# A two-layer transformer trunk on one core: the work ahead of the first projection rebuilt

## What is computed

```python
def ada_modulate(c, w, b):
    m = jax.nn.silu(c) @ w + b
    shift, scale, gate = jnp.split(m, 3, axis=-1)
...
        shift, scale, gate = ada_modulate(c, ada_w[i, 0], ada_b[i, 0])
        h = rms_norm(x, norm_g[i, 0]) * (1.0 + scale) + shift
        ...
            mix = even_mixer(h, rel_bias, ev_w_in[j], ev_w_out[j], ...)
        x = x + gate * mix
```

## Time and profile before

| | us |
|---|---|
| median of 3 runs | 2055.22 |
| lowest and highest run | 2053.96 and 2059.96 |
| span of the profiled execution (first to last instruction) | 2054.0 |
| TensorE busy in it | 1889.3 (92%) |
| VectorE busy in it | 1559.5 (76%) |
| ScalarE busy in it | 1057.0 (51%) |
| first product of `ev_in` starts at | 124.4 |

### The profile page before, as it was taken

One profiled execution on the slowest core, in us unless ns is written; L12 is line 12 of the kernel. 1 busy time (PEld: TensorE's weight loads), 2 busy tenths in 40 slices (PEclk: granted clock), 3 DMA queues, 4 the chain that ended last, 5 costly groups with the idle time before them and its releaser, 6 DMA issues.

```text
span 2054.0 us, 34033 instructions
## 1 busy us (share of the span) xinstructions
PE 1889.3 (92%) x11434; PEld 1629.2 (79%) x11434; DVE 1559.5 (76%) x2447; ACT 1057.0 (51%) x2257; POOL 220.1 (11%) x317
## 2 busy tenths in 40 slices
PE   3279998889999999999999999989999999999998
PEld 2158854766799999997877878777799999998787
DVE  4988744777778888889887888788677777778554
ACT  1145446655544545555544456565455555556443
POOL 2220001552100000000011000043000000000000
PEclk9689998999999999999999999999999999999999
DMA  8979985567588888886997886868567777765555
GB/s 325 399 278 320 339 295 170 198 229 245 200 278 281 270 273 277 278 272 231 331 332 266 271 282 203 301 220 300 193 232 224 225 234 235 224 203 177 177 189 176
DMA packets 210967, 521.25 MB, mean 254 GB/s; under 512 B 23041, under 2 KB 43010, under 8 KB 186018
## 3 DMA queue, kind: packets, MB, share of 16 engines
q1 hardware_dynamic: 180722, 316.19, 47.3%
q0 software_dynamic: 28032, 201.44, 26.9%
q10 hardware_dynamic: 2096, 2.12, 0.3%
HBM read 517.53 MB, written 2.12 MB: 253 GB/s over the span
## 4 chain that ended last, share of the span: by engine, by line
PE 73%; DVE 13%; DMA 9%; ACT 3%; issue 1%; SPq 0%; DVEq 0%; POOLq 0%; ACTq 0%
PE ps L1039 12%; PE ps L1035 12%; PE ps L1036 12%; PE ps L931 10%; PE ps L927 10%; PE ps L928 10%; DVE acc L1712 6%; DVE ring_lo L1790 3%; DMA ring<-in_od_w_in 2%; DMA first_ring<-in_ada_w 2%; DMA ring<-in_ev_w_in 1%; DMA aring<-in_ada_w 1%; PE ps L761 1%; PE ps L1131 1%; DVE L L1947 1%
## 5 line engine op out<-in xcount | busy, mean ns | idle before, releaser
L1242 ACT ACTIVATE ring_hi<-ring 128x512 fp32r<-128x512 f32 (+2 forms) x1152 | 690.8, 621 | 595.5 <-DMA ring<-in_ffn_w_up 231.6
L1790 DVE TENSOR_TENSOR ring_lo<-ring,ring_hi 128x512 fp32r<-128x512 f32 (+2 forms) x1152 | 742.3, 680 | 283.1 <-ACT ring_hi L1242 281.4
L1035 PE MATMUL ps<-hT_hi,ring_hi 128*128 128x256 f32 x2048 | 512.2, 283 | 1.5 <-PE ps L1039 0.7
L1036 PE MATMUL ps<-hT_lo,ring_hi 128*128 128x256 f32 x2048 | 507.2, 280 | 0.0
L1036 PEld LDWEIGHTS ps<-hT_lo,ring_hi 128*128 128x128 f32 x2048 | 387.3, 189 | 0.0
L1035 PEld LDWEIGHTS ps<-hT_hi,ring_hi 128*128 128x128 f32 x2048 | 384.7, 188 | 2.3 <-issue 1.2
L1039 PE MATMUL ps<-hT_hi,ring_lo 128*128 128x256 f32 x2048 | 329.2, 282 | 2.4 <-DVE ring_lo L1790 2.4
L1039 PEld LDWEIGHTS ps<-hT_hi,ring_lo 128*128 128x128 f32 x2048 | 279.2, 187 | 2.6 <-DVE ring_lo L1790 2.6
L1712 DVE SCALAR_TENSOR_TENSOR acc<-aring,cs,acc 128x2048 f32<-128x2048 f32 x112 | 263.4, 2352 | 20.6 <-DMA aring<-in_ada_w 8.8
L928 PE MATMUL ps<-ring_hi,hT_lo 128*128 128x512 f32 (+2 forms) x640 | 243.8, 382 | 0.0
L643 POOL DMA_DIRECT2D aring<-in_ada_w x176 | 94.4, 536 | 1380.7 <-DVE acc L1712 1355.6
(11 more groups left out here) (244 smaller groups left out, 1996.4 us busy)
## 6 DMA issues: line engine op xcount, KB each, us to landing
aring<-in_ada_w POOLq DMA_DIRECT2D x176, 1024.0 KB, 6.9
ring<-in_ffn_w_up SPq DMA_DIRECT2D x512, 256.0 KB, 3.0
ring<-in_ffn_w_down SPq DMA_DIRECT2D x256, 256.0 KB, 3.1
ring<-in_od_w_in SPq DMA_DIRECT2D x112, 256.0 KB, 3.5
ring<-in_ev_w_in SPq DMA_DIRECT2D x80, 256.0 KB, 5.8
first_ring<-in_ada_w POOLq DMA_DIRECT2D x16, 1024.0 KB, 7.2
ring<-in_ev_w_out SPq DMA_DIRECT2D x64, 256.0 KB, 3.5
ring<-in_od_w_out SPq DMA_DIRECT2D x64, 256.0 KB, 4.0
```

Source lines behind the costliest of these rows:

```text
L1035: nc.tensor.matmul(o[q], hi, hT_hi[:, kt, :], start=start, stop=False, skip_group_check=True)
L1036: nc.tensor.matmul(o[q], hi, hT_lo[:, kt, :], start=False, stop=False, skip_group_check=True)
L1242: ins = nc.scalar.activation(out_, in_, f, **kw)
L1790: put(v.tensor_tensor(ring_lo[:, g, part], ring[:, g, part], ring_hi[:, g, part].bitcast(F32), ALU.subtract), lo_ok)
```

## The change

The condition is loaded first on SP and straight as columns (2048 elements of 4 bytes), so that silu(c) needs no turning. GpSimd issues the first four units ahead of the clearing of `acc`. The bias is no longer made with `toeplitz`: the table is split into a high and a low float32r part, stacked to 64 rows, and for each of the 256 key positions a product of 16 columns with a shifted slice of the one-hot table writes one column per head; eight float32 products of 512 columns add the causal mask. The scratch tensor, its two DMAs, `k_neg` and the flipped identity go. SP waits until unit 30 has landed before it issues the first ring buffer. Units 28 to 31 are multiplied by TensorE straight from their buffers, after the column sums of the other 28, into the same accumulators. VectorE's loop is written out, the copies of the parameters stand after unit 7, and the normalised x is made by ScalarE.

```diff
-        FIRST_MOD = 2 * KT
+        FIRST_MOD, DIRECT = 2 * KT, 4
...
+        def first_used(n):
+
+            return first_mod(n) - DIRECT
...
-            row_load(0, ROWS["c"][0], c.rearrange("o (k p) -> (o k) p", p=P))
+            sp.dma_start(cs[:, :], c.rearrange("o (k p) -> p (o k)", p=P), allow_slow_non_contiguous=True).then_inc(c_in, 16)
+            sp.dma_start(hot, k_hot).then_inc(buckets_in, 16)
+            for half in range(2):
+                sp.dma_start(tbl[half * BUCKETS:(half + 1) * BUCKETS, :], rel_bias).then_inc(buckets_in, 16)
...
-            for dst, src in ((con[:, :], k_con), (fold4, k_fold), (hot, k_hot), (negrow, k_neg), (tbl, rel_bias),
+            for dst, src in ((con[:, :], k_con), (fold4, k_fold),
...
+            _, landed_, turn = mod_slot(FIRST_MOD - 2)
+            sp.wait_ge(landed_, 16 * (turn + 1))
             for j, (c0, n) in enumerate(EV_BLOCKS):
                 matrix(KT * j, ev_w_in[0], KT, c0, n)
...
+            for m in range(4):
+                load(m, -1, m % 2, m // 2)
             clear(-1, (0, 1))
-
-            def first_pass(i):
-                for j in range(4):
-                    load(j, -1, j % 2, i * 2 + j // 2, i * 4)
-            first_pass(0)
-            with pool.Fori(1, KT // 2) as i:
-                first_pass(i)
+            for m in range(4, FIRST_MOD):
+                load(m, -1, m % 2, m // 2)
...
-            pe.wait_ge(params_in, 16 * 8)
+            pe.wait_ge(params_in, 16 * 5)
...
-            ins = nc.tensor.matmul(ps[0:SLOTS, 2, 0:REV], tbl[:, :], hotr, start=True, stop=True)
-            lane.done(ins, rev_mm)
-
+            pe.wait_ge(hot_ok.handle, 1)
+            pe.wait_ge(tbl_ok.handle, 2)
...
                     ins = nc.tensor.matmul(ps[:, 3, (t * NCMP + j) * NSA_H:(t * NCMP + j + 1) * NSA_H],
-                                           hotf[:, d0:d0 + P], tbl[:, 0:NSA_H], start=True, stop=True)
+                                           hot_r[:, d0:d0 + P], tbl_r[:, 0:NSA_H], start=True, stop=True)
...
-            pe.wait_ge(toep_in, 16)
-            pe.wait_ge(prm_ok.handle, 4)
-            pe.wait_ge(cb_ok.handle, 1)
-            for b in range(8):
-                ins = nc.tensor.matmul(ps[:, b, :], con[:, C_FLIP:C_FLIP + P], wide[:, b * 512:(b + 1) * 512], start=True, stop=True)
-            lane.done(ins, flipped)
+            def bias_bank(b):
+
+                nc.tensor.matmul(ps[:, b, :].rearrange("p (s h) -> p s h", h=SLOTS), ident,
+                                 causal[:, b * 32:(b + 1) * 32].unsqueeze(2).broadcast_to([P, 32, SLOTS]), start=True, stop=False,
+                                 skip_group_check=True)
+                for s in range(32):
+                    d0 = FWD0 + P - (b * 32 + s)
+                    ins = nc.tensor.matmul(ps[:, b, s * SLOTS:(s + 1) * SLOTS], hot_r[:, d0:d0 + P], tbl_r[:, :],
+                                           start=False, stop=s == 31, skip_group_check=True)
+                lane.done(ins, bias_mm)
+
+            for b in BIAS_BANKS:
+                if b == 0:
+                    pe.wait_ge(prm_ok.handle, 4)
+                if b == 3:
+                    pe.wait_ge(cb_ok.handle, 1)
+                bias_bank(b)
             pe.wait_ge(bias_ok.handle, 8)
...
-                    pe.wait_ge(ada_used.handle, first_mod(n) - 1 + t)
+                    pe.wait_ge(ada_used.handle, first_used(n) - 1 + t)
...
-                                               acc[:, t, j * NB:(j + 1) * NB], start=True, stop=True)
+                                               acc[:, t, j * NB:(j + 1) * NB], start=True, stop=n > 0)
+                if n == 0:
+                    pe.wait_ge(cs_ok.handle, 1)
+                    for m in range(FIRST_MOD - DIRECT, FIRST_MOD):
+                        t, k = m % 2, m // 2
+                        slot, landed_, turn = mod_slot(m)
+                        pe.wait_ge(landed_, 16 * (turn + 1))
+                        for j in range(4):
+                            ins = nc.tensor.matmul(ps[32 * j:32 * j + 1, sums_bank(n) + t, :], cs[:, k:k + 1], slot[:, j * NB:(j + 1) * NB],
+                                                   start=False, stop=k == KT - 1)
...
-            act.wait_ge(ones_ok.handle, 1)
-            act.wait_ge(prm_ok.handle, 4)
-            run(cs_ok, cs[:, :], prm[:, ROWS["c"][0]:ROWS["c"][0] + KT], ACT.Silu)
-
-            act.wait_ge(rev_ok.handle, 1)
-            act.dma_start(toeplitz, rev).then_inc(toep_out, 16)
+            act.wait_ge(c_in, 16)
+            run(cs_ok, cs[:, :], cs[:, :], ACT.Silu)
+            act.wait_ge(buckets_in, 48)
+            run(hot_ok, hot_r, hot, ACT.Copy)
+            run(tbl_ok, tbl_r, tbl, ACT.Copy)
+
             act.wait_ge(x_in, 16)
             for b in range(4):
                 x_squares(b, hT)
             x_norm(0)
-            act.wait_ge(toep_out, 16)
-            act.dma_start(wide[:, 0:SLOTS * S].rearrange("p (h s) -> p h s", h=SLOTS),
-                          bass.AP(toeplitz.tensor, 0, [[1, P], [REV, SLOTS], [1, S]])).then_inc(toep_in, 16)
-            act.wait_ge(flipped.handle, 1)
-            for b in range(8):
-                run(bias_ok, bias[:, 2 * b:2 * b + 2, :], ps[:, b, :].rearrange("p (h s) -> p h s", h=2), ACT.Copy)
+            act.wait_ge(xsd.handle, 2)
+            for b in range(4):
+                cols = slice(b * NB, (b + 1) * NB)
+                for t in range(ST):
+                    run(xn_ok, xn[:, t, cols], x_sb[:, t, cols], ACT.Copy, scale=xst[:, 0, t:t + 1])
+            for i, b in enumerate(BIAS_BANKS):
+                act.wait_ge(bias_mm.handle, i + 1)
+                run(bias_ok, bias[:, :, b * 32:(b + 1) * 32], ps[:, b, :].rearrange("p (s h) -> p h s", h=SLOTS), ACT.Copy)
...
-            dve.wait_ge(cs_ok.handle, 1)
...
-                def one_pass(i):
-                    lane.after()
-                    put(v.tensor_copy(cs_now[:, 0:2], cs[:, 0:2] if isinstance(i, int) else cs[:, bass.ds(i * 2, 2)]))
-                    for j in range(4):
-                        mod_unit(j, j % 2, cs_now[:, j // 2:j // 2 + 1], i * 4)
-                one_pass(0)
+                def units(m0, m1):
+                    for m in range(m0, m1):
+                        mod_unit(m, m % 2, cs[:, m // 2:m // 2 + 1])
+
+                dve.wait_ge(cs_ok.handle, 1)
+                units(0, 1)
+                dve.wait_ge(tbl_ok.handle, 1)
+                put(v.tensor_tensor(tbl_r[BUCKETS:, :], tbl[BUCKETS:, :], tbl_r[BUCKETS:, :].bitcast(F32), ALU.subtract), tbl_ok)
+                units(1, 8)
...
+                dve.wait_ge(prm_T.handle, 1)
+                for a, b in ((0, ROWS_A), (PE_COL, PE_COL + 2 * CMP_BLOCK), (CW_COL, 4 * P), (4 * P, PRM)):
+                    put(v.tensor_copy(prm[:, a:b], ps[:, a // 512, a % 512:a % 512 + b - a]), prm_ok)
...
+                units(8, 12)
                 normed(0)
-                with lane.loop(1, KT // 2, {ada_used: 4, dve_s: 1}, ada_used) as i:
-                    one_pass(i)
+                units(12, FIRST_MOD - DIRECT)
...
+                if n == 0:
+                    return
                 lane.after()
                 for b in range(4):
-                    for t in range(ST if n == 0 or b >= 2 else 1):
+                    for t in range(ST if b >= 2 else 1):
```

54 lines of the change are left out of this document (21 added, 33 removed).

## The result

| | before | after |
|---|---|---|
| median (4 runs each, same chip) | 2054.7 us | 2043.76 us |
| lowest and highest run | 2053.96 and 2059.96 | 2040.8 and 2050.84 |
| span of the profiled execution | 2054.0 | 2049.1 |
| first product of `ev_in` | 124.4 | 115.4 |
| from there to the end of the span | 1929.6 | 1933.7 |

The ratio is 0.9943 with a 95% interval of 0.9921 to 0.9966, that is 7.0 to 16.2 us. A second session with 7 and 19 runs gave 0.9944, 0.9917 to 0.9971 (2045.79 against 2055.51), and there the first product stood at 116.0. The profiled execution of the changed kernel is its slowest of the first four; the other spans were 2042.8, 2041.3 and 2039.1. So the prologue is read by its first product, and the span of that one execution is not used.

A forecast was written before the change was run, and what follows sets the result against it. TensorE's bias work was to set the prologue's end: 22.5 + 1.8 + 6.5 + 68.8 = 99.6 us, then 0.5 + 2.6 + 7.4 + 0.3 = 110.4 against 117.4. Saving 7.0 gave span 2047.0, median 2048.2 us; range 2043 to 2060.

The forecast's parts named there:

- the six groups behind the bias: TensorE after the bias: two groups of column sums and four direct units, 7.4 us, partly at the lower clock.
- The start of TensorE: Prologue: parameters landed and TensorE starting at 22.5 us, with 3.2 us for the condition; 26.0 at 53 ns per element.
- the mask product: TensorE's bias: one product of 512 columns per bank, taken as 1.7 us; eight banks 68.8 us.
- the stretch behind the first product: Rest of the kernel after the first `ev_in` product: shifts as one piece, its length kept to 2 us.
- the distance of the device time from the span: Whole kernel: the median stands 1.2 us above the profiled span, turning 2047.0 into 2048.2 us.
- Small products: TensorE's bias: small products 0.215 us each at 1.2 GHz, 32 of them 6.9 us per bank.
- Copy to first product: End of the prologue: first `ev_in` product 7.0 us after the sums, as before; sums near 110, product near 117.4.
- DMA end: DMA engines: modulation units finished at 100.0 us instead of 112.1, including 3.2 us added for the condition.
- ScalarE's gate: ScalarE before copying the sums: six high parts, their buffers issued after unit 30, done at 105.7 us; next thing late.
- the first: Rival on TensorE's bias: clock rises, bias over by 63 us, gain 11.7 us, time 2043.5; chance 0.20.
- The second: Rival on early loads: parameters or condition elements delayed beside unit packets, TensorE late, 2058.1 to 2062; chance 0.16.
- The third: Rival on prologue: dearer condition elements or small products, bias ends 4 to 7 us later, 2052 to 2055; chance 0.14.

The follow-up runs named there:

- the one with the stalls: Changed kernel with half the mask products, sums copied ahead of the high parts and all 32 units on VectorE: 2058.53 us, ratio 0.9991 to before.

## Why the prediction was right in mechanism and wrong in the size of its terms

The chain it named is the chain that came: DMA units early, VectorE at 90, TensorE's bias over near 99.6, sums copied after it. What failed is the size of its terms: its sum was 7.0 us, and the prologue gave 8.9 and the medians 10.9. In the prologue the step that failed is the term for the six groups behind the bias, 7.4 us, which measured 5.75; it holds 1.7 of the 1.9 us. The start of TensorE and the mask product were each missed by more, and cancelled. Outside the sum, the prediction took two things as fixed that moved: the stretch behind the first product, and the distance of the device time from the span. Step by step:

- **Start of TensorE: the largest single error.** 22.5 was forecast, 19.61 came. The condition was priced at 3.2 us by 25 ns an element; alone it costs 9.5 ns, 1.2 us. The 25 ns had been averaged from the earlier trace rows, packets among which larger ones stood, and the choice between 25 and 53 ns looked only upwards. The remaining 0.9 us is the stretch of 17.0 taken over from before; no run divides it.
- **Small products: right.** 0.216 apart, as the earlier trace rows had it. The rule cited there, the Trainium skill, "TensorE: Matmul & The Clock Gate", section "LDWEIGHTS (loading the stationary operand)", of 107 ns for 128 columns does not hold at this level: the 256 products of the bias came at twice that.
- **The mask product: too cheap.** 1.7 was taken, since line 860's 1.14 held a rising clock; 2.00 came. A bank is 8.93, eight are 71.4 against 68.8. This and the early start cancelled: 99.6 was forecast for the end of the bias, 99.2 came. That was luck: 2.9 us too late at the start and 2.6 too few in the eight banks.
- **Six groups behind the bias: too dear.** 7.4 us against 5.75, from 102.66 to 108.41. The forecast carried 4.7 us of low clock from line 860, counted from the first group. By the durations the clock rose earlier, while the column sums ran: two groups took 2.32, where the direct ones behind them took 0.86 each and 1.7 is the lower level's price. The three microseconds of turns ahead of them may have counted, since on line 860 no work stood ahead; no run tests it. Nor is the moment fixed: the same two groups took 2.99 us in the changed kernel's second trace and 1.96 to 3.56 in other kernels that had the same turns ahead. The term was taken as one number and scatters by 1.6 us.
- **Copy to first product**: 7.0 forecast, 6.95 came. **DMA end**: 100.0 forecast, 97.5 came (kernel without direct units); 2.0 of the 2.5 us are the element price. **ScalarE's gate**: 105.7 forecast, 103.5 came.
- **Behind the first product** the forecast kept the stretch's length to 2 us and called itself wrong in its base otherwise. It was 1929.6 before, 1933.7 after and 1926.1 in the changed kernel again; in the others it went from 1920 to 1937 in no order of what was edited (1948 in the one with the stalls). One kernel's two traces differ by 7.6 us, so single traces can't decide that sign, and the premise of a fixed stretch was finer than the kernel is.
- **From span to median** the forecast added 1.2 us, the distance between a span and the median of other executions. Where one execution has both, the device time was 2.09 to 2.17 us over the span before and 1.63 to 1.76 in the changed kernels: 0.4 us of the 10.9 lie outside the span. The cause is open. The remaining 1.6 us, between the 8.9 of the prologue and the medians, lie inside the scatter of the stretch and inside the interval of the ratio; no run shows a cause for them.

Of the rivals, the first gave nearly the number that came (2043.5), by coincidence and not by its mechanism: products didn't follow at 0.11, and it was ScalarE that waited 5.00 us for TensorE. The second was shown to be one transfer away. The third didn't come.

## What to carry to other kernels

Put transfers of many tiny elements first, before any queue holds large packets: the same 2048 elements cost 1.2 us there and 14 behind. Before moving work from one engine to another, ask which of the two is late at that place: the same four units cost 2.3 us and then, once TensorE's list had been shortened, earned 3.2. When a shortened list brings less than it was shortened by, read what stands ahead of the next step on the engine that copies its result; here it was six casts for which no one was waiting yet.

## What the runs showed that was not expected

- 2048 elements of 4 bytes: landed 3.0 to 3.4 us after issue as the first transfer of all, 4.1 as a second such transfer, 15.3 beside 8 KB packets.
- 128 shifted copies of 16 KB (2 MB): 14.7 us to landing before, 44.5 and 43.6 in the two kernels with the old bias. Before, GpSimd asked for no unit from 38.2 to 47.4 us, just as they began; there its units ran beside them all the time. That this is the reason was not tested.
- A small packet and an 8 KB packet of two queues were taken one for one: 165 and 165, then 168 and 168, in 3 us each.
- At the lower clock a product of 256 columns took 0.2225 us and one of 16 columns 0.216: columns up to there are nearly free, and filling them with zeros did not raise the clock in 70 us.
- The granted clock of a stretch read 1.00 through all 70 us of the bias, while its products ran at the pace of the 1.2 GHz level.
- Products with one weight column are no cheaper than those with 32: in the kernel without the mask four of them side by side took 1.04 us, and a group of four column sums 1.07.
